# A transformer block's first mixer: the low parts of four weight units by a transfer that adds, and the convolution's last taps moved from TensorE to VectorE

## What is computed

```python
h = rms_norm(x, norm1_g[l])
proj = h @ w_in[l]                                   # 1024 x 2560
q, k, v, u = jnp.split(proj, [ATTN_WIDTH, 2 * ATTN_WIDTH, 3 * ATTN_WIDTH], axis=-1)
q = apply_rope(rms_norm(q, q_norm_g[l]), cos, sin)   # 8 heads of 64, k alike
attn = moba_attention(q, k, v)                       # one block of 256: causal attention
# conformer_conv(u): GLU, causal depthwise convolution, layer norm, silu
a, g = jnp.split(u + glu_b, 2, axis=-1)
h = a * jax.nn.sigmoid(g)                            # 512 channels
h = conv(pad(h, 30 rows), dw_w) + dw_b               # 31 taps for each channel
conv = jax.nn.silu(layer_norm(h, ln_g, ln_b))
x = x + jnp.concatenate([attn, conv], axis=-1) @ w_out[l]
```

## Time and profile before

| | us |
|---|---|
| median of three runs (lowest, highest) | 1285.66 (1285.11, 1286.18) |
| span of the profiled execution | 1283.5 |
| PE busy | 1273.1 |
| DVE busy | 840.7 |
| ACT busy | 676.6 |
| POOL busy | 110.3 |
| first mixer, from unit 4 to the start of `rows(2, 0)` | about 36 to 107 of the span |

### The profile page before, as it was taken

How to read it: one execution, slowest core, us unless ns; L and a number is a source line. 1 busy time by engine, 2 the same in 40 slices (tenths; PEclk the granted TensorE clock), 3 DMA queues, 4 the chain that set the end, 5 groups by cost and what they waited for, 6 DMA issues and landing times.

```text
span 1283.5 us, 18290 instructions
## 1 busy us (share of the span) xinstructions
PE 1273.1 (99%) x7066; PEld 1088.3 (85%) x7066; DVE 840.7 (65%) x1114; ACT 676.6 (53%) x905; POOL 110.3 (9%) x128
## 2 busy tenths in 40 slices
PE   9999999999999999999999999999999999999998
PEld 8978888888888888887888888888888877888886
DVE  7997665565655548898765556655556776665553
ACT  6776554443544435656564444544454665564441
POOL 2761000000000000022000000000002120000000
PEclk9999999999999999999999999999999999999999
...
GB/s 314 134 89 199 253 205 196 196 213 117 242 203 187 186 152 120 176 85 244 197 230 183 184 190 163 202 258 196 192 186 127 245 159 166 148 236 185 182 150 33
DMA packets 175055, 234.94 MB, mean 183 GB/s; under 512 B 4608, under 2 KB 154896, under 8 KB 174993
## 3 DMA queue, kind: packets, MB, share of 16 engines
...
q0 software_dynamic: 2896, 8.65, 2.1%
...
...
HBM read 233.03 MB, written 1.05 MB: 182 GB/s over the span
## 4 chain that ended last, share of the span: by engine, by line
PE 93%; POOL 3%; DVE 1%; issue 1%; ACT 1%; DMA 0%; DVEq 0%; POOLq 0%; ACTq 0%
PE psum L1239 23%; PE psum L1135 14%; PE psum L1136 14%; PE psum L1137 14%; PE psum L1247 12%; PE psum L1260 2%; PE psum L1202 2%; PE psum L1201 2%; PE psum L1200 2%; POOL ws L1059 2%; PE psum L1264 1%; PE psum L1472 1%; PE psum L1363 1%; PE psum L1520 1%; PE psum L1485 1%
## 5 line engine op out<-in xcount | busy, mean ns | idle before, releaser
L1911 DVE TENSOR_TENSOR w_lo<-raw,w_hi 128x2048 fp32r<-128x2048 f32 x197 | 448.7, 2283 | 82.7 <-ACT w_hi L499 81.1
L499 ACT ACTIVATE w_hi<-raw 128x2048 fp32r<-128x2048 f32 x211 | 401.5, 1907 | 31.6 <-PE psum L1137 11.7
L1239 PE MATMUL psum<-t_both,w_hi 128*128 128x512 f32 x1280 | 304.7, 390 | 0.0
L1239 PEld LDWEIGHTS psum<-t_both,w_hi 128*128 128x128 f32 x1280 | 237.4, 188 | 47.4
L1135 PE MATMUL psum<-w_hi,f_hi 128*128 128x512 f32 x488 | 192.7, 395 | 0.0
L1137 PE MATMUL psum<-w_hi,f_lo 128*128 128x512 f32 x488 | 190.2, 390 | 0.0
L1136 PE MATMUL psum<-w_lo,f_hi 128*128 128x512 f32 x488 | 190.1, 389 | 0.0
L1135 PE MATMUL psum<-w_hi,t_both 128*128 128x512 f32 (+2 forms) x464 | 165.6, 357 | 0.0
L1137 PE MATMUL psum<-w_hi,t_both 128*128 128x512 f32 (+2 forms) x464 | 162.3, 350 | 0.0
L1136 PE MATMUL psum<-w_lo,t_both 128*128 128x512 f32 (+2 forms) x464 | 162.3, 350 | 0.0
L1247 PEld LDWEIGHTS psum<-t_both,w_lo 128*128 128x128 f32 x1280 | 158.9, 192 | 3.1
...
## 6 DMA issues: line engine op xcount, KB each, us to landing
raw<-in_ffn_wg SPq DMA_DIRECT2D x44, 1024.0 KB, 5.6
raw<-in_ffn_wu SPq DMA_DIRECT2D x44, 1024.0 KB, 5.4
raw<-in_ffn_wd SPq DMA_DIRECT2D x44, 1024.0 KB, 5.0
raw<-in_even_w_in SPq DMA_DIRECT2D x12, 1024.0 KB, 5.2
raw<-in_odd_w_in SPq DMA_DIRECT2D x12, 1024.0 KB, 6.0
raw<-in_w_gate SPq DMA_DIRECT2D x11, 1024.0 KB, 5.6
raw<-in_w_up SPq DMA_DIRECT2D x11, 1024.0 KB, 5.7
raw<-in_w_down SPq DMA_DIRECT2D x11, 1024.0 KB, 5.0
```

Of the source, the lines that this page charges most:

```text
L499: nc.scalar.activation(w_hi[:, n % SLOTS, 0:w], raw_of(n)[:, 0:w], ACT.Copy).then_inc(hi_done, 1)
L1239: mm = nc.tensor.matmul(bank[b + c][:, :], wh[:, k, c * P:(c + 1) * P], t_both[:, k, :, :].rearrange("p a s -> p (a s)"), start=k == 0 and ...
L1911: nc.vector.tensor_tensor(w_lo[:, n % SLOTS, 0:w], raw_of(n)[:, 0:w], w_hi[:, n % SLOTS, 0:w].bitcast(F32), ALU.subtract).then_inc(lo_done, 1)
```

## The change

Units 7 to 10 get their low parts in another way: ACT writes the negated rounded weights (`negated(n)`) into `w_lo`, and POOL issues a transfer that reads the unit once more from memory and adds it to what stands there (`low_part(n)`). DVE makes no low part of them. PE waits for the transfer's own semaphore (`low_ready`), and a `raw` buffer is free again once ACT has read it for the negation. The last 11 taps of tile 3 move from PE to DVE, with a sum of their own in bank 2; tiles 0 and, from its seventh tap, 2 get two sums each, in banks 6 and 2, that take the taps in turn and are joined by `tap_sum`. POOL builds no diagonals. The orders of all four engines in `mix_first` are new; the bodies of the moved steps become functions. The diff, cut (lines that only replace a wait by `low_ready`, that only wrap a step in a function, and removed lines of the orders are left out):

```diff
                          t1=g_row[:, 0:512], t2=g_row[:, 512:1024], qr=g_pre.rearrange("p (b t n) -> p b t n", b=2, t=T),
-                         diag=wv(9080, 8, P))
+                         side=wv(9080, S))
...
-        ACT_CT, ACT_PE = 1, 3
+        ACT_CT, SIDE_CT = 1, 3
         SINGLES = 11
-        PE_TAPS = range(20, TAPS)
-        PIECES = [(tap, min(tap + 4, TAPS)) for tap in range(PE_TAPS.start, TAPS, 4)]
+        SIDE_TAP = 20
         DVE_TAPS = []
-        for ct in map(int, "0000000000000" "20202" "202" "20" "20202" "202" "20" "20" "202022022" "20220" "202" "20220" "20222"):
-            DVE_TAPS.append((sum(c == ct for _, c in DVE_TAPS), ct))
+        for ct in map(int, "0" * 13 + "03" * 11 + "02" * 7 + "2" * 24):
+            DVE_TAPS.append((sum(c == ct for _, c in DVE_TAPS) + SIDE_TAP * (ct == SIDE_CT), ct))
+        LOW_ADDED = (7, 8, 9, 10)
+        def low_ready(n, turn=0):
+            if n in LOW_ADDED:
+                return low_in[LOW_ADDED.index(n)], 16
+            return lo_done, n + 1 - sum(m <= n for m in LOW_ADDED) + turn * SLOTS
         block = stack.enter_context(nc.Block())
...
                     sp.wait_ge(xn_ready, 2 * T)
                 elif n > SPARE:
-                    sp.wait_ge(lo_done, n - RAWS + (n > 2 * RAWS) + SLOTS * turn)
+                    last = n - RAWS - (n <= 2 * RAWS)
+                    sp.wait_ge(*((minus_hi, LOW_ADDED.index(last) + 1) if last in LOW_ADDED else low_ready(last, turn)))
                 sp.dma_start(raw_view(n, width, by_rows), src).then_inc(raw_landed(n)[0], 16)
             def load_tables():
...
+            def negated(n):
+                nc.scalar.activation(w_lo[:, n % SLOTS, :], raw_of(n), ACT.Copy, scale=-1.0).then_inc(minus_hi, 1)
             def first_half():
...
                 split_to(7)
+                taps(2)
                 split_to(8)
+                taps(1)
+                negated(7)
                 taps(3)
                 square(4)
                 split_to(9)
+                negated(8)
+                taps(3)
                 square(5)
+                taps(1)
+                split_to(10)
                 taps(2)
                 keep_rope(units[4][3], 7)
+                square(6)
+                keep_rope(units[5][3], 7)
                 taps(1)
+                negated(9)
+                exps(L, 0)
                 taps(1)
                 split_to(11)
                 keep_unit(ph, 7)
+                keep_pt(L, 0)
+                exps(L, 1)
                 taps(2)
                 keep_rope(units[6][3], 7)
+                exps(L, 2)
                 taps(1)
+                keep_pt(L, 1)
                 square(8)
+                taps(2)
+                lam_exps()
                 exps(L, 3)
+                negated(10)
+                keep_rope(units[8][3], 7)
                 keep_pt(L, 2)
                 taps(2)
                 keep_pt(L, 3)
+                keep_sums(0, V["inv"][0])
                 exps(L, 4)
                 exps(L, 5)
+                taps(1)
                 keep_pt(L, 4)
                 taps(1)
+                keep_pt(L, 5)
+                exps(L, 6)
+                taps(1)
                 group_hi(0, 6, scaled=True)
+                keep_unit(ph, 9)
                 taps(1)
                 exps(L, 7)
                 keep_pt(L, 6)
+                taps(2)
+                keep_pt(L, 7)
                 split_to(12)
+                split_to(13)
                 keep_sums(5, V["inv"][1])
+                centred_squares(0)
+                centred_squares(1)
...
+                silu_table()
+                swish(0)
+                swish(1)
...
+                    def low_part(n):
...
+                        i = LOW_ADDED.index(n)
...
+                        pool.wait_ge(minus_hi, i + 1)
+                        pool.dma_start(dst, src, accum_op=ALU.add).then_inc(low_in[i], 16)
...
+                    add(5)
+                    low_part(7)
+                    add(2)
                     root(0)
+                    add(5)
+                    low_part(8)
+                    add(1)
                     root(1)
                     add(3)
+                    low_part(9)
                     root(2)
+                    add(6)
                     root(3)
+                    low_part(10)
+                    add(8)
                     pool.wait_ge(rope_T, 4)
...
+                def spread_sums(lo, b):
+                    if lo == 0:
+                        pe.wait_ge(bank_free[0], left[8])
+                    else:
+                        pe.wait_ge(pt_kept, L["h0"] + 8)
+                    group_spread(L, lo, b)
...
+                tile(4, 0)
+                tile(4, 1)
+                tile(5, 0)
+                tile(5, 1)
+                tile(6, 0)
+                turned(4)
+                tile(6, 1)
+                turned(5)
+                tile(7, 0)
+                scores(0)
+                tile(7, 1)
+                scores(2)
+                turn(0)
+                tile(8, 0)
+                turn(1)
+                turned(6)
+                tile(8, 1)
+                tile(9, 0)
+                turn(2)
+                spread_sums(0, 0)
+                turned(8)
+                values(0)
+                scores(4)
+                turn(3)
+                tile(9, 1)
+                values(2)
+                turn(4)
+                scores(6)
+                turn(5)
+                turn(6)
+                values(4)
                 rows(0, 0, (0,))
                 turn(7)
                 rows(0, 0, (1,))
                 values(6)
...
+                mean()
+                spread_sums(4, 5)
                 rows(0, 1)
...
+                variance()
                 rows(1, 0, (0,))
...
+                spread_root()
+                rows(1, 1, (0,))
                 rows(1, 0, (1,))
+                rows(1, 1, (1,))
                 rows(2, 0)
                 rows(3, 0)
                 rows(2, 1)
...
-                    split_lo(cur[0], widths.get(cur[0], UC))
+                    if cur[0] not in LOW_ADDED:
+                        split_lo(cur[0], widths.get(cur[0], UC))
                     cur[0] += 1
...
+                    sums = {(0, 0): bank[6][:, 0:S], (0, 1): bank[6][:, S:2 * S], (2, 0): bank[2][:, 0:S], (2, 1): bank[2][:, S:2 * S], (3, 0): bank[2][:, S:2 * S]}
                     for tap, ct in DVE_TAPS[at[0]:at[0] + n]:
                         src, w = V["hpad"][:, ct, tap:tap + S], tap_col[:, 4 * tap + ct:4 * tap + ct + 1]
-                        acc = bank[2][:, ct // 2 * S:(ct // 2 + 1) * S]
-                        final = (tap + 1, ct) not in DVE_TAPS
+                        one = (ct, tap % 2 if ct == 0 or ct == 2 and tap > 6 else 0)
+                        acc = sums[one]
                         if tap == 0:
                             ins = nc.vector.tensor_scalar(acc, src, w, p_col[:, DW_B + ct:DW_B + ct + 1], ALU.mult, ALU.add)
+                        elif one not in last:
+                            if one == (2, 1):
+                                dve.wait_ge(dve_step, last[3, 0])
+                            ins = nc.vector.tensor_scalar(acc, src, w, None, ALU.mult)
                         else:
-                            dve.wait_ge(dve_step, last[ct])
-                            ins = nc.vector.scalar_tensor_tensor(out=V["acc"][:, ct, :] if final else acc, in0=src, scalar=w, in1=acc,
+                            dve.wait_ge(dve_step, last[one])
+                            final = tap == TAPS - 1
+                            ins = nc.vector.scalar_tensor_tensor(out=(V["side"] if ct == SIDE_CT else V["acc"][:, ct, :]) if final else acc, in0=src, scalar=w, in1=acc,
                                                                  op0=ALU.mult, op1=ALU.add)
-                        if final:
-                            ins.then_inc(conv_ok, 1)
-                        else:
-                            last[ct] = step(ins)
+                        last[one] = step(ins)
                     at[0] += n
...
+                def tap_sum(ct):
+                    dve.wait_ge(dve_step, max(last[ct, 0], last[ct, 1]))
+                    nc.vector.tensor_tensor(V["acc"][:, ct, :], bank[6 if ct == 0 else 2][:, S:2 * S], V["acc"][:, ct, :], ALU.add)                        .then_inc(conv_ok, 1)
...
+                    dve.wait_ge(tap_added, TAPS - 1)
+                    nc.vector.tensor_tensor(V["acc"][:, SIDE_CT, :], V["side"], V["acc"][:, SIDE_CT, :], ALU.add).then_inc(side_ok, 1)
...
                 split_to(4)
                 glu(1)
+                taps(3)
                 split_to(5)
+                taps(2)
+                split_to(6)
+                taps(3)
+                split_to(7)
+                taps(1)
+                setup()
+                taps(4)
+                glu(3)
+                mean_square(0)
+                lam_sums()
+                rope_begin(4)
```

(38 more changed lines are left out.)

292 lines of the change are left out of this document (98 added, 194 removed).

## The result

The changed kernel takes 1289.2 us (median of 10 runs, 1286.4 to 1290.8), the kernel before 1285.56 us beside it (1285.11 to 1286.69). The ratio is 1.0024, 95% interval [1.0016, 1.0033]: 0.24% slower, where I had forecast 0.25% faster. The profiled execution took 1290.12 us, 0.9 above the median, with a span of 1288.3 us.

What follows compares the result with a forecast made beforehand. TensorE, busy 99% of the span, was taken to bound the kernel, with DVE full in the first mixer's windows. The root spread 3.2 us earlier gave 1285.66 - 3.2 = 1282.5 us, range 1279.5 to 1288.

Steps and rivals of the forecast that it cites:

- (5): TensorE's own way through the first mixer: some 4.8 us of new waits, so rows(0, 0) begins at 87.
- (3): DVE's new waits before `side`: 3.0 us of the 5.1 go again, and `side` ends at about 91.5.
- (4): From `side` to the rows of units 12 and 13: root spread at 99.2 against 102.38, 3.2 us earlier.
- (1): TensorE loses tile 3's convolution pieces: 5.1 us that nothing hides; with 2.5 us of waits, 7.6 at most.
- (2): DVE's work before `side`: loses four low parts, gains 11 alternating taps and two joins; net -5.1 us.
- (6): ACT gains four negations, 7.3 us pitched, and has room for them.
- (7): Adding transfers: land in 11.4 us, making unit 9 about 1 us late; issuing one holds POOL 0.58 us.
- rival C: Adding transfers run at a quarter of the rate, 18 us, and TensorE waits for them: 1289 us; chance 0.15.
- rival D: POOL's issue takes many us rather than 0.58, holding taps and roots, and ends as B; chance together 0.20.
- B: Waits eat the gain: DVE held 1 to 3 us more, 1283.5 to 1286 us; chance with rival D 0.20.
- (8): POOL's additions, slowed up to 2 us each by the four low parts, are relieved; last tap ready at 91.2.

Runs made afterwards that it cites:

- e1: Changed kernel with 25 matmuls that nothing reads (12, 6, 5 and 2) put into four of TensorE's waits; 1286.2 us, ratio to the kernel before 1.0006.
- e3: Kernel before, with 8 of the 11 convolution taps on TensorE left out, so the output is not the reference's; 1286.5 us, ratio 1.0004.
- e6: Changed kernel, unit 8's transfer three additions earlier on POOL, unit 4's keep_rope right after square(5) on ACT, and unread matmuls in TensorE's waits; 1284.55 us.
- e11: e6 with five taps of tile 3 back on TensorE in place of seven fillers, and unit 10's low part back on DVE; 1286.0 us.
- e4: Kernel before, with only unit 10's low part made by ACT's negation and an adding transfer instead of DVE's subtraction; 1286.85 us, ratio 1.0014.
- e2: Changed kernel, with unit 8's adding transfer issued three additions earlier on POOL; 1288.92 us.
- e7: e6 without fillers, values(4) ahead of turn(6) on TensorE, four ACT steps ahead of exps(6), and DVE's group_lo(0, 6) five taps earlier; 1285.72 us.

## Why the prediction was wrong, step by step

Two steps failed, and their prices are about equal. The forecast was 1282.5 us, the result 1289.2, which is 6.7 us.

"The clock is 1.00 in all the windows, so it stays out of the sum": this was true of the kernel before only, whose convolution passes stood between the waits. I had listed 4.8 us of new waits in (5) and not asked what they do to the clock. Price: 3.0 us (e1).

"`side` ends at about 91.5", in (3), and the root with it in (4): with the clock held the root still comes 3.8 us later than I had it, and the time is no better than before the change. What failed is the 3.0 us of waits for DVE; with the clock held (e1) they are 6.4.

(1) 5.1 us of passes, "nothing hides them": they went, but what they were worth was not their length. In the kernel before, e3 took 3.7 us away and gained none. The 2.5 us of waits beside them, which I took as removable with them, grew instead.

(2) The count of DVE's work was right in kind: the low parts are gone, the taps alternate at 0.39 to 0.40 us (seven from 48.92 to 51.66), and DVE has gaps.

(3) and (4) I had `side` at 91.5 us, 41.2 counted from the turn of unit 4. With the clock held (e1) it ends at 94.36, or 44.9: 3.7 us late. DVE waits 3.56 us for the square of unit 4 (3.40 in the changed kernel), where I had 1.4, since I let the square start at 41.88, when TensorE ends the unit, and didn't see that ACT's taps ahead of it wait for POOL behind POOL's issue. Further waits are 0.45, 0.66, 1.47 and 0.30 us, where I had 0.4 and 1.2. The hold (2.41 us for 0.17) comes on top, but in e6, without it, `side` still ends at 44.2, and waits of 0.47 and 0.66 us for ACT's squares have come in its place. No run moved unit 7's transfer, so what the wait for the square costs in time is read from the traces and not measured. The root came at 52.66, where I had 48.9 (the terms of (4) add up to 99.1, not 99.2; that changes nothing).

(5) The late waits came as sized: 1.48 for 1.5, 1.21 for 1.5, 0.67 for 0.4. `turned(5)` was mis-sized: 3.37 for 0.6, since I had DVE undisturbed and didn't see bank 7 waiting for ACT. With the clock held, rows(0, 0) begins at 40.2 counted from the turn of unit 4, where I had 36.7: 3.5 us late. This wait is 2.8 us longer than I had it, but e6, in which `turned(5)` comes 1.8 us earlier, gained only 0.7 us at rows(0, 0). The root's 3.8 us and the clock's 2.8 to 3.0 add up to the 6.7 us between 1282.5 and 1289.2.

(6) Four negations of 1.90 us; that of unit 10 is hidden in the changed kernel (e11), as I said, and all but 0.27 us of it in the order of the kernel before (e4). That of unit 7 isn't: POOL waits 2.21 us for it.

(7) The transfers landed as estimated, and nobody waited for them, so rival C didn't come:

```profile
w_lo<-in_w_in POOLq DMA_DIRECT2D x3, 1024.0 KB, 10.7
...
w_lo<-in_w_out POOLq DMA_DIRECT2D x1, 1024.0 KB, 10.6
```

(KB each, median us from issue to landing; my estimate was 11.4.) But their issue held POOL longer than the 0.58 us of the earlier trace rows:

```profile
L1094 POOL TENSOR_TENSOR ws<-ws 128x512 f32<-128x512 f32 x19 | 25.5, 1340 | 10.1 <-ACT ws L753 9.1
...
L1108 POOL DMA_DIRECT2D w_lo<-in_w_in x3 | 4.9, 1646 | 2.9 <-ACT w_lo L517 2.9
```

That is 6.1 us in all against 2.3, which was rival D's mechanism in small: it held taps, at 41.89 us in the changed kernel and at 79.97 us in e4. I had given B with D, whose time was 1283.5 to 1286 us, a chance of 0.20. Its sign, DVE idle for over 4 us before `side`, came (6.4 us), and with the clock held the kernel takes 1286.2 us, at the upper end; the result lies above that by the clock.

(8) POOL's additions were relieved as forecast, 1340 ns in the mean against 1497 in the kernel before, none over 1.90 us. POOL still ended late, through its issues and its waits for ACT's taps (9.1 us).

The page "SBUF — State Buffer" of the Trainium skill (Who interferes with whom) says that `tensor_scalar` can take both of DVE's port pairs, one of which it shares with GpSimd, and that whoever comes second is blocked for the whole instruction. I used this page for the relief in (8) and not against the issues of (7). The trace agrees with a block of that kind: DVE is released 0.02 and 0.03 us after the end of POOL's addition in the two kernels shown, and 0.03 us after it in the kernel before. It differs in one thing: the hold of 2.4 us lasts over two instructions of POOL, the issue and the addition; which of them holds DVE at first isn't shown.

The page "TensorE: Matmul & The Clock Gate" of the Trainium skill (HAM oscillation — how this bites in real kernels) says that gaps in TensorE's work bring the clock down in the middle of a kernel. The trace agrees: 0.50 behind the wait of 3.37 us, and again behind three waits of 3.36 us in all. But not every such gap does it here: the clock is 1.00 behind a wait of 2.99 us in e2 and behind waits of 0.67, 1.49 and 0.74 us in e7.
